# The final norm with tokens on partitions, its transposes and squares moved beside the last down projection

## The reference

```
def rmsnorm(x, g):
    xf = x.astype(jnp.float32)
    y = xf * lax.rsqrt(jnp.mean(xf * xf, axis=-1, keepdims=True) + EPS)
    return (y * g.astype(jnp.float32)).astype(x.dtype)

def sqrelu_mlp(h, w1, w2):
    return jnp.square(jax.nn.relu(h @ w1)) @ w2

        h = h + sqrelu_mlp(rmsnorm(h, mlp_norm[layer]), mlp_w1[layer], mlp_w2[layer]).astype(h.dtype)
    return rmsnorm(h, final_norm)
```

## Time and profile before

| what | value |
|---|---|
| median of 3 runs | 1265.14 us (1264.33 to 1265.75) |
| profiled execution, whole | 1264.38 us |
| its span | 1262.6 us |
| TensorE matmuls busy | 1225.1 us, 97% of the span |
| VectorE busy | 901.1 us, 71% |
| ScalarE busy | 716.5 us, 57% |
| GpSimd busy | 250.7 us, 20% |
| mean HBM traffic | 165 GB/s |
| last matmul of the down projection ends | 1246.87 us from the span's start |

### The profile page before, as it was taken

One profiled execution on the slowest core, in us unless ns is written; L12 is line 12 of the kernel. 1 busy time (PEld: TensorE's weight loads), 2 busy tenths in 40 slices (PEclk: granted clock), 3 DMA queues, 4 the chain that ended last, 5 costly groups with the idle time before them and its releaser, 6 DMA issues.

```text
span 1262.6 us, 24148 instructions
## 1 busy us (share of the span) xinstructions
PE 1225.1 (97%) x8266; PEld 1118.6 (89%) x8266; DVE 901.1 (71%) x1548; ACT 716.5 (57%) x1301; POOL 250.7 (20%) x269
## 2 busy tenths in 40 slices
PE   7999989999999999999999999999999999999996
PEld 5988889999999988888889888888889998888885
DVE  5778875555557988875667868786658878887564
ACT  4657755664444556654446776664445787666341
POOL 3000022220000114430120003441004511443010
PEclk9999999999999999999999999999999999999998
DMA  7413335555556556655574436655556434665530
GB/s 219 156 35 130 102 101 167 170 195 167 199 173 223 190 169 199 199 173 194 166 222 146 134 101 200 190 177 199 169 165 199 137 118 150 200 196 172 198 133 33
DMA packets 202388, 207.19 MB, mean 164 GB/s; under 512 B 6079, under 2 KB 199605, under 8 KB 202185
## 3 DMA queue, kind: packets, MB, share of 16 engines
q1 hardware_dynamic: 200053, 203.12, 50.4%
q10 hardware_dynamic: 2260, 3.09, 0.8%
HBM read 205.12 MB, written 2.63 MB: 165 GB/s over the span
## 4 chain that ended last, share of the span: by engine, by line
PE 87%; DVE 5%; ACT 4%; issue 3%; DMA 0%; DVEq 0%; ACTq 0%; SPq 0%; POOLq 0%; POOL 0%
PE PS L1801 31%; PE PS L1802 16%; PE PS L1795 11%; PE PS L1796 10%; PE PS L1797 10%; DVE wlo L1016 1%; PE PS L2017 1%; PE PS L1952 1%; ACT whi L514 1%; PE PS L1995 1%; ACT x L548 1%; DVE tmp L1037 1%; PE PS L2111 0%; PE PS L2109 0%; PE PS L2110 0%
## 5 line engine op out<-in xcount | busy, mean ns | idle before, releaser
L1016 DVE TENSOR_TENSOR wlo<-raw,whi 128x1024 fp32r<-128x1024 f32 x370 | 454.8, 1237 | 178.6 <-ACT whi L514 177.0
L514 ACT ACTIVATE whi<-raw 128x1024 fp32r<-128x1024 f32 x370 | 389.3, 1054 | 328.4 <-PE PS L1802 215.5
L1801 PE MATMUL PS<-x,whi 128*128 128x512 f32 x832 | 291.4, 394 | 0.0
L1801 PE MATMUL PS<-hid,whi 128*128 128x512 f32 x768 | 268.0, 395 | 0.2
L1795 PE MATMUL PS<-x,whi 128*128 128x258 f32 (+2 forms) x864 | 252.2, 292 | 6.8 <-DVE x L993 5.8
L1796 PE MATMUL PS<-x,whi 128*128 128x258 f32 (+2 forms) x864 | 248.2, 287 | 0.0
L1797 PE MATMUL PS<-x,wlo 128*128 128x258 f32 (+2 forms) x864 | 246.4, 285 | 0.0
L1802 PE MATMUL PS<-x,wlo 128*128 128x256 f32 x832 | 234.4, 282 | 0.0
L1802 PE MATMUL PS<-hid,wlo 128*128 128x256 f32 x768 | 213.2, 278 | 0.0
L1683 POOL TENSOR_TENSOR acc<-acc,sq 128x256 f32<-128x256 f32 (+2 forms) x72 | 59.2, 823 | 685.0 <-ACT sq L552 341.9
L1801 PEld LDWEIGHTS PS<-x,whi 128*128 128x128 f32 x832 | 156.3, 188 | 36.0
(11 more groups left out here) (301 smaller groups left out, 1713.5 us busy)
## 6 DMA issues: line engine op xcount, KB each, us to landing
raw<-in_mlp_w SPq DMA_DIRECT2D x64, 1024.0 KB, 5.4
raw<-in_w_mlp_up SPq DMA_DIRECT2D x32, 1024.0 KB, 5.5
raw<-in_w_mlp_down SPq DMA_DIRECT2D x32, 1024.0 KB, 5.1
raw<-in_w_in_conv SPq DMA_DIRECT2D x12, 1024.0 KB, 5.2
raw<-in_attn_w_in SPq DMA_DIRECT2D x12, 1024.0 KB, 5.2
raw<-in_mlstm_w_in SPq DMA_DIRECT2D x12, 1024.0 KB, 5.3
raw<-in_w_in_attn SPq DMA_DIRECT2D x9, 1024.0 KB, 5.7
raw<-in_w_out_attn SPq DMA_DIRECT2D x4, 1024.0 KB, 5.3
```

Of the source, the lines that this page charges most:

```text
L514: A(part_view(whi, b), raw_view(b), ACT.Copy).then_inc(w_hi, 1)
L1016: V.tensor_tensor(part_view(wlo, b), raw_view(b), f32(part_view(whi, b)), ALU.subtract).then_inc(w_lo, 1)
L1801: mm(dst.rearrange("p (a t) -> p a t", a=2), std_cols(whi[b % RING], k), xs_both, start=first, stop=False)
```

## The change

The final norm is turned around. Once a tile of `h` is complete, TensorE transposes its two squares of 128x128 (one per half of the tokens, a = 0 and 1) into PSUM banks 4 to 7: `o_bank`, tiles 0 to 3 in banks 4 and 6, tiles 4 to 7 in banks 5 and 7. ScalarE squares each transposed piece and gets the sum over its 128 features with it (`accum_out`), and VectorE multiplies each piece with the gain, from PSUM into `o_tok`. The two engines take turns: a = 0 for ScalarE while VectorE has a = 1, and then the other way round. The table `outs_at(q, late)` says behind which block q a tile's part is issued: TensorE transposes tiles 0 to 5 behind blocks 8, 9, 16, 17, 24 and 25 (`late` 1); ScalarE and VectorE take them at steps 9, 10, 17, 18, 25 and 26 (`late` 2); tiles 6 and 7 come after the last block. A tile that goes into banks in use first waits until the tile before it has been read by both engines (`out_n` and `out_sq`). At the end the sums of a token are added, rstd is made for 128 tokens by 2 numbers, and each half of the tokens is scaled with its rstd as a factor per partition, the left 512 columns by ScalarE and the right by VectorE, and stored. The gain is loaded once, spread over all partitions (512 KB), by ScalarE's queue before the last MLP. TensorE's loop of two passes is written out in the last down projection. The norm's GpSimd part is gone.

```diff
+            o_tok, o_gain = sb("o_tok", [P, TS, D], F32, s), sb("o_gain", [P, D], F32, s)
+            o_sq, o_sums, o_st = sb("o_sq", [P, TS, P], F32, s), sb("o_sums", [P, TS, KB], F32, s), sb("o_st", [P, 3, TS], F32, s)
...
+        def o_bank(o, a):
+
+            return 4 + 2 * a + o // 4
+
+        def outs_at(q, late):
+
+            return [o for o in range(KB - 2) if 8 * (o // 2) + 7 + o % 2 + late == q]
...
+            def out_squares(o):
+
+                for a in range(TS):
+                    act.wait_ge(Z["out_t"], o + 1)
+                    if a:
+                        act.wait_ge(Z["out_n"], TS * o + 1)
+                    A(o_sq[:, a, :], PS[:, o_bank(o, a), (o % 4) * P:(o % 4 + 1) * P], ACT.Square, accum_out=o_sums[:, a, o:o + 1])\
+                        .then_inc(Z["out_sq"], 1)
...
                         if j < 15:
                             split_hi(B[dn] + j + RING + (16 * i if m == 3 else 0), 0 if m == 3 else i, 16)
-                        if j % 8 >= 6:
+                        if m == 3:
+                            for o in outs_at(16 * i + j, 2):
+                                out_squares(o)
+                        elif j % 8 >= 6:
                             o = 2 * (j // 8) + j % 8 - 6
-                            if m == 3:
-                                residual(8, 4 * i + o, tok, (Z["h_ready"], 8 * m + 4 * i + o + 1))
-                            else:
-                                residual(2 * m + 2, o, tok, (Z["h_ready"], 8 * m + o + 1), i)
+                            residual(2 * m + 2, o, tok, (Z["h_ready"], 8 * m + o + 1), i)
...
+            act.wait_ge(w_used, B["up3"])
+            act.dma_start(o_gain[:, :], bass.AP(d["v_rows_b"].tensor, row_b["final_norm_2"] * P, [[0, P], [1, D]]))\
+                .then_inc(Z["out_gain_in"], 16)
             mlp(3, LAST)
-            norm(8, LAST)
+            for o in (KB - 2, KB - 1):
+                out_squares(o)
+            act.wait_ge(Z["out_ss"], 1)
+            A(o_st[:, 1, :], o_st[:, 0, :], ACT.Ln, bias=eps[:, 0:1], scale=1.0 / D).then_inc(Z["out_ln"], 1)
+            act.wait_ge(Z["out_ln"], 1)
+            A(o_st[:, 1, :], o_st[:, 1, :], ACT.Exp, scale=-0.5).then_inc(Z["out_ln"], 1)
+            act.wait_ge(Z["out_rs"], 1)
             for a in range(TS):
-                act.wait_ge(Z["out_t"], 2 * a + 1)
-                A(x_tok[:, a, 0:512], PS[:, 2 * a, :], ACT.Copy).then_inc(Z["out_left"], 1)
+                A(o_tok[:, a, 0:512], o_tok[:, a, 0:512], ACT.Copy, scale=o_st[:, 1, a:a + 1]).then_inc(Z["out_left"], 1)
...
+            def out_evict(o):
+
+                cols = slice(o * P, (o + 1) * P)
+                dve.wait_ge(Z["out_t"], o + 1)
+                if o == 0:
+                    dve.wait_ge(Z["out_gain_in"], 16)
+                for a in (1, 0):
+                    if a == 0:
+                        dve.wait_ge(Z["out_sq"], TS * o + 1)
+                    mul(o_tok[:, a, cols], PS[:, o_bank(o, a), (o % 4) * P:(o % 4 + 1) * P], o_gain[:, cols]).then_inc(Z["out_n"], 1)
...
+                        if m == 3:
+                            for o in outs_at(16 * c + j, 2):
+                                out_evict(o)
...
-            norm(8, LAST)
-            dve.wait_ge(Z["sq_ready"], 9 * KB)
-            for k in range(KB):
-                stt(at(h, k, LAST), at(h, k, LAST), gain(8, k), rstd[:, 0:S], ALU.mult, ALU.mult).then_inc(Z["out_n"], 1)
+            for o in (KB - 2, KB - 1):
+                out_evict(o)
+            dve.wait_ge(Z["out_sq"], TS * KB)
+            V.tensor_reduce(o_st[:, 0, :], o_sums[:, :, :], mybir.AxisListType.X, ALU.add).then_inc(Z["out_ss"], 1)
+            dve.wait_ge(Z["out_ss"], 1)
+            dve.wait_ge(Z["out_ln"], 2)
+            V.tensor_scalar(o_st[:, 2, :], o_st[:, 0, :], 1.0 / D, EPS, ALU.mult, ALU.add).then_inc(Z["out_step"], 1)
+            dve.wait_ge(Z["out_step"], 1)
+            mul(o_st[:, 2, :], o_st[:, 2, :], o_st[:, 1, :]).then_inc(Z["out_step"], 1)
+            dve.wait_ge(Z["out_step"], 2)
+            mul(o_st[:, 2, :], o_st[:, 2, :], o_st[:, 1, :]).then_inc(Z["out_step"], 1)
+            dve.wait_ge(Z["out_step"], 3)
+            V.tensor_scalar(o_st[:, 2, :], o_st[:, 2, :], -0.5, 1.5, ALU.mult, ALU.add).then_inc(Z["out_step"], 1)
+            dve.wait_ge(Z["out_step"], 4)
+            mul(o_st[:, 1, :], o_st[:, 1, :], o_st[:, 2, :]).then_inc(Z["out_rs"], 1)
+            dve.wait_ge(Z["out_rs"], 1)
             for a in range(TS):
-                dve.wait_ge(Z["out_t"], 2 * a + 2)
-                V.tensor_copy(x_tok[:, a, 512:D], PS[:, 2 * a + 1, :]).then_inc(Z["out_right"], 1)
+                V.tensor_scalar(o_tok[:, a, 512:D], o_tok[:, a, 512:D], o_st[:, 1, a:a + 1], None, ALU.mult).then_inc(Z["out_right"], 1)
...
-            sums(8, S)
...
                         last.then_inc(w_used, 1)
+                        if m == 3:
+                            for o in outs_at(16 * i + j, 1):
+                                out_transposes(o)
+
+                if m == 3:
+                    for i in range(2):
+                        down(i)
+                else:
+                    with pe.Fori(0, 2) as i:
+                        down(i)
+
+            def out_transposes(o):
+
+                pe.wait_ge(Z["h_ready"], 3 * KB + o + 1)
+                if o == 0:
+                    pe.wait_ge(Z["norm_read"], 8)
+                elif o % 4:
+                    pe.wait_ge(Z["out_n"], TS * o)
+                    pe.wait_ge(Z["out_sq"], TS * o)
+                for a in range(TS):
+                    c = o * T + N_META + a * P
+                    last = nc.tensor.transpose(PS[:, o_bank(o, a), (o % 4) * P:(o % 4 + 1) * P], h[:, c:c + P], ident[:, :])
+                last.then_inc(Z["out_t"], 1)
...
-            norm(8, S)
-            pe.wait_ge(psum_read, total)
-            for a in range(TS):
-                for f in range(KB):
-                    pe.wait_ge(Z["out_n"], f + 1)
-                    last = nc.tensor.transpose(PS[:, 2 * a + f // 4, (f % 4) * P:(f % 4 + 1) * P],
-                                               h[:, f * T + N_META + a * P:f * T + N_META + (a + 1) * P], ident[:, :])
-                    if f % 4 == 3:
-                        last.then_inc(Z["out_t"], 1)
+            for o in (KB - 2, KB - 1):
+                out_transposes(o)
 
 
 _OUT = (1, SEQ, D)
```

More of the change, by code:

```diff
@@ L257, in build @@
             relu_done dn_scaled out_half cs_ready const_set pool_set pro_t pro_ev h_ready x_hi x_ready sq_ready acc_ready norm_mm norm_ln norm_read rstd_ready
-            y_hi y_ready hid_hi hid_sq hid_ready dve_step out_n out_t out_left out_right out_sent
+            y_hi y_ready hid_hi hid_sq hid_ready dve_step out_n out_t out_sq out_ss out_ln out_rs out_step out_gain_in out_left out_right out_sent
             c_hi c_lo c_sq c_sum c_row c_ln gq_set fg_abs fg_ln fg_rows fg_sent
@@ L497, in _ @@
                 sp.wait_ge(Z["out_right"], a + 1)
-                sp.dma_start(out[0, a * P:(a + 1) * P, :], x_tok[:, a, :]).then_inc(Z["out_sent"], 16)
+                sp.dma_start(out[0, a * P:(a + 1) * P, :], o_tok[:, a, :]).then_inc(Z["out_sent"], 16)
             sp.wait_ge(Z["out_sent"], 16 * TS)
@@ L1860, in mlp, with down @@
                 norm(2 * m + 1, tok[1])
-                with pe.Fori(0, 2) as i:
+                def down(i):
                     for j in range(16):
```

## The result

| | before | after |
|---|---|---|
| median, us | 1264.88 (1263.82 to 1266.64, 17 runs) | 1268.53 (1266.0 to 1272.0, 17 runs) |
| ratio after / before | | 1.0031, 95% interval 1.0023 to 1.0039 |
| profiled execution, us | 1264.38 | 1268.33 |
| its span, us | 1262.6 | 1266.5 |
| end of the last down projection's last matmul to the end of the span, us | 15.7 | 10.6 |

A forecast was written before the change was run, and what follows sets the result against it. TensorE was taken as the down projection's only bound, with a chain behind its last matmul. Transposes +1.6, stalls +6.0, end -5.7 and clock +1.5 made +3.4 us on 1265.14: 1268.5 us, range 1264.8 to 1272.5.

The forecast's parts named there:

- end: Behind the last down projection's last matmul (M): the span ends at M+10.0 instead of M+15.7, a gain of 5.7 us.
- six pairs of transposes: Inside the last down projection: twelve transposes between matmuls cost 0.26 us a pair, 1.6 us in all.
- three stalls: Behind blocks 9, 17 and 25: TensorE waits for readers of the banks, 2.0 us each, 6.0 in all.
- clock: In the last down projection: the stalls make TensorE's clock fall, +1.5 us; bounds none and two at 3.0 each.
- small steps: At the end, between squares and scalings: sum, logarithm, exponential and five small VectorE steps take 1.7 us, to M+5.2.
- bounds of 9.4 and 10.9: Span's end behind M: 9.4 with small steps of 0.12 and uncontended stores; 10.9 with squares not overlapping or stores hindering.
- one fall at half price: Behind one of the three stalls: the clock falls once, at half the 3.0 us of an earlier row, +1.5 us.
- the clock holds: Rival, at all three stalls: the clock does not fall, +1.9 us in all, 1267.0 us; chance 38%.
- full price of 3.0 us: Loss from a clock fall at an earlier wait (185.2 us): 6.0 us of matmuls at half speed, 3.0 us lost.
- forecast's own range: Whole kernel: 1266.9 to 1270.7 us for the forecast case itself, given a chance of 44%.
- At nothing: Gain load, VectorE's products and the loop written out in the last down projection: taken to cost nothing.

The follow-up runs named there:

- e2: Changed kernel with the odd tiles transposed one block later, squares and products a step later too; 1262.54 us, ratio 0.9978 to the kernel before.
- e8: Kernel before, last down projection written out, with the change's six pairs of transposes added and read by nothing; 1266.92 us, ratio 1.0011.
- e0: The changed kernel run once more, unaltered, as reference and for a second profile; 1268.82 us, ratio 1.0037 to the kernel before.
- e1: Changed kernel with ScalarE's squares of a tile put ahead of the split of the same step; 1262.65 us, ratio 0.9983 to the kernel before.
- e3: Kernel before, last down projection written out, three TensorE waits added for the low weights three blocks on; 1278.32 us, ratio 1.0101.
- e5: Kernel before, last down projection written out, three TensorE waits added for the high weights three blocks on; 1271.23 us, ratio 1.0045.
- e9: Kernel before, last down projection written out, six unread transposes at each of six places, 36 in all; 1269.03 us, ratio 1.0028.
- e4: Kernel before with TensorE's last down projection written out instead of looped, nothing else; 1265.11 us, ratio 0.9998.
- e6: Changed kernel with tiles 1 and 3 transposed a block later, tile 5 as in the change; 1264.81 us, ratio 0.9996 to the kernel before.

## Why the prediction was right, point by point

The forecast of 1268.5 us met the median of 1268.53. The mechanism is the forecast one, but that the two agree to 0.03 us is luck: the median of the kernel before lies 0.26 us under the one from which the forecast was counted, and of the terms the end is 0.6 us and the transposes 0.3 above the forecast, the clock, as estimated below, 0.4 to 0.8 under it. The terms against what was measured:

| term, us | forecast | measured |
|---|---|---|
| end | -5.7 | -5.1 |
| six pairs of transposes | +1.6 | +1.9 (7.88 - 6.0); +2.24 without stalls (e2, e8) |
| three stalls | +6.0 | +6.0 (the next start 2.00 us later each time) |
| clock | +1.5 | none in the first profile, one fall of 1.5 in that of e0 |
| sum | +3.4 | +2.8 and, in e0, +4.6; medians +3.65 |

*The stalls.* Place, cause and length were right: three, behind blocks 9, 17 and 25, each ended by VectorE's product, resume at E+1.84 as worked out. TensorE's transposes start at 1189.12, where without the wait they would have started 0.12 behind the last matmul's start of 1187.00: 2.00 us later, as forecast, and the same at the other two. Net of what the transposes cost in e2 a stall comes to 1.88, because behind two of the three the pace was the faster one. That the stalls are what turns the sign was shown from both sides: taken away by either of two edits, the ratio falls from 1.0037 to 0.9983 and 0.9978 (e1, e2); put alone into the kernel before, they slow it (e3, e5).

*The transposes.* The slots were right (0.22 measured for 0.26), but the sum left out a slower pace of the matmuls behind them, 0.9 us in all in e2 and e8 and some 0.5 in the change. The record of each still reads 0.27 us as a duration. The Trainium skill's price ("TensorE: Matmul & The Clock Gate", Part 4, about 275 ns for a transpose), taken as spacing, would have made 36 of them 9.9 us, an estimate from that page; the 36 of e9 cost 4.3 at a clock of 1.00, so as a spacing it does not hold here.

*The end.* Each step came a little late: transposes of tile 7 at M+2.46 for 2.4, squares done at M+3.66 for 3.5, scalings started at M+5.53 for 5.2, the span's end 3.7 behind the last scaling for 3.45. Of the 0.6 us the squares make 0.2, the small steps 0.1 (1.84 measured from their first start to the scalings, 1.7 forecast), and the stores, the largest part, 0.3. It makes M+10.6, within the bounds of 9.4 and 10.9. Before, the span ended 3.15 us behind the last copy; with two stores of 512 KB at once it ends 3.74 behind the last scaling, 0.6 more and not 0.3. Windows behind the last scaling,

```profile
1263.00:1264.00 1.00, 0.00 (x0) 0.00 (x0) 0.00 (x0) 0.00 (x0) 0.00 (x0) 0.50 0.97 389
1264.00:1265.00 1.00, 0.00 (x0) 0.00 (x0) 0.00 (x0) 0.00 (x0) 0.00 (x0) 0.50 1.04 422
1265.00:1266.00 1.00, 0.00 (x0) 0.00 (x0) 0.00 (x0) 0.00 (x0) 0.00 (x0) 0.50 0.62 238
```

with the 16 DMA engines full at 389 and 422 GB/s for the first two. That the stores hinder each other fits this; no run has them apart in the new end.

*The clock.* The forecast's "one fall at half price" was the weakest step, and its reason for the half did not hold: a fall costs 1.5 us in full here, in four of four (e0, e3), and it does not come every time. The first profile has none, and so is the case of the rival "the clock holds" (+1.9), with a sum of +2.8; that of e0 has one. How often the clock falls in the runs without a profile can be estimated in two ways. The mean granted clock that goes with each run is 0.0010 lower in e0 than in e1 and e2, where one fall of 3.4 us would make 0.0013; and the medians of e0 and e2 are 6.3 us apart, the stretches without a fall 5.6. Both point to half a fall to one a run, some +0.7 to +1.1 us. The full price of 3.0 us was too high for this stretch. (The forecast's own range should have begun at 1265.14 + 2 = 1267.1, not 1266.9.) The Trainium skill ("TensorE: Matmul & The Clock Gate", "Why this matters for your kernels") would have waits of this size leave the clock alone: that agrees with e5 at 1.25 us, and not with e3 at 2.5 us, nor with one of the three stalls of 1.8 us in e0.

*At nothing.* The loop written out: shown (e4). The gain load and the products on VectorE: no wait of TensorE for weights stands in the down projection of after.

## What to carry to other kernels

When work is moved beside a stream that one engine bounds, follow each new wait of that engine back through the queue of the one it waits for: if what it needs stands behind an instruction that itself waits for the bounding engine, the stall is paid in full each time, and one block later, or ahead of the other engine's own wait, it costs nothing (e2) or some 0.2 us (e1). Count the small operations put into a dense matmul stream by how far they shift the next start, not by their duration, and look at the pace behind them too. Price such a stall with its clock: three of three of 2.5 us added 1.5 us each.

## What was not expected of the hardware

Between the same matmuls at a granted clock of 1.00 two paces exist, 0.347 and 0.353 us for a pair. Before, in e4 and in e5, the whole stretch runs at the first, even behind the stalls of e5. With a pair of transposes inserted it is mostly the second (behind five of six places in e8), and a further pair or a stall can bring back the first; in e3 it became the second with no transposes at all. What sets it is not known.

Longer waits in this stretch were more often followed by a fall of the clock: none of three at 1.25 us (the profile of e5), one in seven at 1.8 us (three in each of two profiles, one in e6), three of three at 2.5 us (e3). These are few, each length but 1.8 us is from one profile, and elsewhere in the kernel a wait of 2.6 us left the clock at 1.00; so the length of the wait alone doesn't decide it.
